# Attention heads of a two-layer block: a chunk's values and the emptying of their bank ahead of the slot's scores, in every engine's queue

## What is computed

```
def mla_attend(qn, qr, kn, kr, v):                       # 8 heads, kind "A"
    s = einsum('bqhd,bkhd->bhqk', qnb, kn) + einsum('bqhr,bkr->bhqk', qrb, kr)
    p = softmax(s * scale); return einsum('bhqk,bkhe->bqhe', p, v)
def diff_attend(q1, q2, k1, k2, v, lam):                 # 4 heads, kind "B"
    p = softmax(q1 k1^T * scale) - lam * softmax(q2 k2^T * scale)
    return einsum('bhqk,bkhe->bqhe', p, v)
for l in range(2):
    o_a = mla_attend(latent queries, context + latent keys)      # 768 keys
    o_b = diff_attend(latent queries, context + latent keys)
    if l == 0:  the same for the 256 context queries over 256 context keys
    o = branches, gates, w_out; then a convolutional feed-forward
```

## Time and profile before

| | |
|---|---|
| median of 3 runs | 3942.68 us (3940.96 to 3946.26) |
| the profiled execution | 3944.44 us, span of its instructions 3942.7 us |
| TensorE busy / VectorE / ScalarE | 89% / 48% / 37% of the span |
| mean granted TensorE clock | 0.938 of 2.4 GHz |
| heads of layer 0 | from about 150 to 636 us |
| heads of layer 1 | from about 1509 to 1967 us |

### The profile page before, as it was taken

How to read it: one execution, slowest core, us unless ns; L and a number is a source line. 1 busy time by engine, 2 the same in 40 slices (tenths; PEclk the granted TensorE clock), 3 DMA queues, 4 the chain that set the end, 5 groups by cost and what they waited for, 6 DMA issues and landing times.

```text
span 3942.7 us, 42589 instructions
## 1 busy us (share of the span) xinstructions
PE 3510.4 (89%) x17750; PEld 2934.2 (74%) x17750; DVE 1892.3 (48%) x2667; ACT 1443.6 (37%) x2201; POOL 312.0 (8%) x244
## 2 busy tenths in 40 slices
PE   7788998999999986788779999888999976979997
PEld 6667777888888875677667888766887765857886
DVE  5554555747635335445555645435333455334233
ACT  4443444233324243334423323434232344253222
POOL 0000000211001100000011101111001200230001
PEclk9999999999999998899899999999999867989999
DMA  5001014423321120011163332221222200212221
GB/s 194 33 19 57 32 54 156 157 96 123 109 79 65 59 73 32 5 57 45 64 219 128 124 109 90 92 78 67 98 100 91 77 1 11 79 51 86 101 91 65
DMA packets 74495, 321.96 MB, mean 82 GB/s; under 512 B 8896, under 2 KB 17856, under 8 KB 52288
## 3 DMA queue, kind: packets, MB, share of 16 engines
q1 hardware_dynamic: 74304, 319.25, 23.6%
HBM read 303.49 MB, written 15.73 MB: 81 GB/s over the span
## 4 chain that ended last, share of the span: by engine, by line
PE 68%; DVE 15%; ACT 9%; issue 3%; DMA 3%; POOL 2%; SPq 1%; POOLq 0%; ACTq 0%; DVEq 0%
PE psum L647 19%; PE psum L648 19%; PE psum L649 19%; DVE arena L1502 2%; DVE split_weights L618 2%; DMA arena<-w_ada_dram 2%; DVE arena L1434 2%; PE psum L1145 2%; ACT arena L1278 1%; POOL arena L1934 1%; ACT split_weights L607 1%; DVE split_high L1448 1%; PE psum L660 1%; PE psum L1171 1%; PE psum L661 1%
## 5 line engine op out<-in xcount | busy, mean ns | idle before, releaser
L647 PE MATMUL psum<-split_inputs,split_weights 128*128 128x512 f32 (+1 forms) x2936 | 1088.5, 371 | 18.8 <-DVE split_weights L618 14.4
L648 PE MATMUL psum<-split_inputs,split_weights 128*128 128x512 f32 (+1 forms) x2936 | 1076.8, 367 | 0.0
L649 PE MATMUL psum<-split_inputs,split_weights 128*128 128x512 f32 (+1 forms) x2936 | 1075.6, 366 | 0.0
L618 DVE TENSOR_TENSOR split_weights<-arena,split_weights 128x2048 fp32r<-128x2048 f32 (+3 forms) x246 | 508.1, 2067 | 405.7 <-ACT split_weights L607 405.4
L647 PEld LDWEIGHTS psum<-split_inputs,split_weights 128*128 128x128 f32 x2936 | 561.3, 191 | 115.3 <-DVE split_weights L618 16.3
L648 PEld LDWEIGHTS psum<-split_inputs,split_weights 128*128 128x128 f32 x2936 | 560.6, 191 | 90.9 <-issue 4.2
L649 PEld LDWEIGHTS psum<-split_inputs,split_weights 128*128 128x128 f32 x2936 | 559.5, 191 | 89.2
L607 ACT ACTIVATE split_weights<-arena 128x2048 fp32r<-128x2048 f32 (+3 forms) x246 | 413.6, 1682 | 176.4 <-PE psum L649 163.7
L647 PE MATMUL psum<-split_hidden,split_weights 128*128 128x512 f32 (+1 forms) x880 | 324.6, 369 | 0.6 <-DVE split_weights L618 0.5
L648 PE MATMUL psum<-split_hidden,split_weights 128*128 128x512 f32 (+1 forms) x880 | 324.3, 369 | 0.0
L649 PE MATMUL psum<-split_hidden,split_weights 128*128 128x512 f32 (+1 forms) x880 | 324.2, 368 | 0.0
(11 more groups left out here) (316 smaller groups left out, 5000.8 us busy)
## 6 DMA issues: line engine op xcount, KB each, us to landing
arena<-w_up_dram SPq DMA_DIRECT2D x44, 1024.0 KB, 4.8
arena<-ffn_up_dram SPq DMA_DIRECT2D x44, 1024.0 KB, 4.8
arena<-w_ada_dram SPq DMA_DIRECT2D x80, 512.0 KB, 3.8
arena<-w_in_dram SPq DMA_DIRECT2D x32, 1024.0 KB, 4.9
arena<-w_down_dram SPq DMA_DIRECT2D x32, 704.0 KB, 4.2
arena<-ffn_down_dram SPq DMA_DIRECT2D x32, 704.0 KB, 4.1
arena<-od_w_in_dram SPq DMA_DIRECT2D x13, 1024.0 KB, 4.9
arena<-w_ada_dram SPq DMA_DIRECT2D x8, 1024.0 KB, 12.7
```

What stands on the lines that cost most here:

```text
L618: dve.e.tensor_tensor(ws[:, i, 1, 0:nk * w], raw_view(key), ws[:, i, 0, 0:nk * w].bitcast(F32), ALU.subtract).then_inc(*w_lo(*key))
L647: pe.e.matmul(dst, a[0], b[0], start=i == 0, stop=False)
L648: pe.e.matmul(dst, a[0], b[1], start=False, stop=False)
L649: ins = pe.e.matmul(dst, a[1], b[0], start=False, stop=i == n - 1)
```

## The change

In the loop over slots, the two lines that emit a slot's first score and the weighing move from ahead of the values to behind them (and so behind `ob_sum`). Nothing is added or removed.

```diff
@@ head_items, for x, (i, c) in enumerate(slots) @@
         scores = plan[x]["scores"]
-        out += scores[0:1]
-        out += [("weigh", t) for t in weigh]
-        weigh = [t for _, t in scores if t in second]
         of_norm(x, "ob_sum")
         values.append((i, c))
         if len(values) > 2:
             of_values(x, *values.pop(0))
+        out += scores[0:1]
+        out += [("weigh", t) for t in weigh]
+        weigh = [t for _, t in scores if t in second]
         of_norm(x, "ob_root")
         out += gates[x]
```

## The result

The changed kernel takes **3876.98 us** (median of 4 runs, 3872.85 to 3878.43) against 3944.01 of the kernel before in the same comparison: ratio 0.9834, 95% interval 0.9821 to 0.9846, 67 us faster. The forecast was 3884 in a range of 3866 to 3914. The profiled execution took 3875.62 us, its span is 3873.9, 68.8 less than before, at a mean granted clock of 0.944.

The account below looks back on a forecast made before the run. With no engine full in layer 1's kind A heads, a loop through several engines, with TensorE waiting at L1171 for the bank, sets the pace; 31 + 5 + 10 + 13 = 59 us gained, forecast 3884 us, range 3866 to 3914.

Parts of the forecast that it names:

- the signs: Profile readings expected after the change, such as L1171's waits for L1460 falling from 77 to about 30 us.
- the three waits of 2.5: TensorE's three alike waits in layer 0's kind B, to be filled by L1171 and values: 6.6 us, each below 1.3.
- Kind A, layer 1: Heads of 27.1 us fall to 19.9 at full or 22.9 at half clock: 31 us gained (23 to 39).
- the emptying: ScalarE's bank copy and VectorE's two instructions after it, moved ahead of exponential and maximum: bank free 2.3 us earlier a pair.
- Kind A, layer 0: Heads of 24.0 us gain a net 0.8 each, ScalarE and VectorE handing to each other binding: 5 us (2 to 8).
- (a): ScalarE's and VectorE's part: bank freed ahead of exponential and maximum, 2.3 us earlier a pair, these two 0.86 us later.
- Kind B, layer 0: TensorE nearly full; values fill its waits, with some work behind them at full clock: 10 us gained (6 to 13).
- Kind B, layer 1: The 6.10 us wait shortens by 3.3, waits for L1465 go, values fill score waits: 13 us gained (8 to 17).
- Rival 1: In the heads, stretches behind shortened waits stay at half clock: 45 us gained, 3898 us; chance 0.23.
- Rival 2: The exponential becomes the bound everywhere, as in layer 0's kind A: 20 us gained, 3923 us; chance 0.14.
- Rival 3: Some 110 scores come late behind values and the emptying gains nothing: 15 us slower at most, 3958 us; chance 0.06.
- Rival 4: No change: the stage behind the heads takes their gain back, waiting for a DMA or a weight; chance 0.05.

Follow-up runs that it names:

- e2: Kernel before with only ScalarE's and VectorE's queues changed (bank emptied ahead of exponential and maximum), TensorE's order kept: 3905.78 us, ratio 0.9901.
- e4: Kernel before with all three queues changed, but only in layer 1's kind A slots: 3911.59 us, ratio 0.9912.
- e7: Changed kernel, but VectorE takes the maximum first as before and TensorE keeps the score ahead of values that begin a pair: 3904.88 us, ratio 0.9901.
- e5: Changed kernel, but on TensorE alone a slot's first score stays ahead of values that begin a pair: 3894.59 us, ratio 0.9872.
- e1: Kernel before with only TensorE's queue changed (values ahead of the score): 3961.62 us, ratio 1.0043.
- e6: Kernel before with only TensorE's queue changed, the score staying ahead of values that begin a pair: 3946.25 us, ratio 1.0011.
- e9: Changed kernel, but in layer 0's kind A VectorE takes the maximum first and TensorE keeps the score ahead of pair-beginning values: 3876.65 us, ratio 0.9830.
- e3: Changed kernel, but VectorE keeps its order of before, the maximum ahead of the two instructions that free the bank: 3908.77 us, ratio 0.9910.

## Why the prediction was right, and where not

- **The sum.** 59 us forecast, 67 measured, all four terms on the low side, none by more than 3.4. Most of the signs came: L1171's waits at 35.6 for about 30, layer 1's heads at 20.9 with a clock of 0.93, layer 0's at 23.1, the three waits of 2.5 at 1.3; VectorE's waits for scores, 25.4 in all, stayed below 30, and ScalarE waited at L1298 once, for 0.65 us.
- **Kind A, layer 1** (31 forecast, 33.2): right in kind and size. e2 shows that the emptying alone makes it, e4 that it is made within the stage. Heads take 20.9 us where 19.9 and 22.9 were reckoned at the full and the half clock. The clock rose to 0.93: 13.9 us of the 32.1 in that stretch.
- **Kind A, layer 0** (5, measured 6.4): the size right, the reason half right, and part of it luck. The net of 0.8 us a head does not follow from the numbers given with it: 1.05, less twice 0.86 with 0.4 given back, is 0.13. That an exponential later by the emptying costs time there is what e7 against e5 shows, 0.83 us each with the clock's part in it. But I took TensorE's order for harmless there; e1 and e6 show that alone it costs 20 us, since L1171 stands ahead of the score, and that (a) turns it into a gain (6.1, e5) once the wait is short.
- **Kind B, layer 0** (10, measured 13.4): the waits went as forecast (1.31, 1.35 and 1.35 left of the three of 2.50; the one of 7.2 became 7.99), idle time fell by 7.3 against some 9 reckoned. The mis-sized term is the clock behind the filled waits: 0.9 us forecast in all, 6.1 measured. e5 shows that it is the values in the waits that gain: without a pair's first values there, the stage has -4.2.
- **Kind B, layer 1** (13, measured 15.7): the wait of 6.10 became 2.70, 3.4 shorter against 3.3; those for L1465 outside the tail are gone. Idle time fell by 9.3 where about 12 was reckoned, and the clock again gave more, 6.4 against about 1.
- **Rival 1** (half clock) fell: it would have left kind A's stretch in layer 1 at 0.81. **Rival 2** (the exponential binds everywhere) fits kind A of layer 0 alone. **Rival 3** names a harm that is real in TensorE's order alone, of nearly that size, but by another way: e1 lies at 3962 where it said 3958, not by the length of the values ahead of 110 scores but by a waiting instruction ahead of two scores in a head. In the change its condition, an emptying that gains nothing, did not hold. It also took VectorE to wait for scores at about 9 places in layer 0; the kernel before has 6, with 12.2 us. **Rival 4** (no change) fell: the stretch between the layers moved by -0.4.
- **The change as two parts that add** was wrong. -18.9 and 43.3 do not make 68.3. The forecast did not use the sum of the two: it walked both parts together, stage by stage.

## What to carry to other kernels

When an item moves ahead of another in an in-order queue, ask what it waits for, not only how long it runs: the same swap was worth +6 or -20 us with the wait in front of it short or long. An edit to a shared list is several edits, one for each engine, and their gains need not add; try them apart before keeping or dropping the whole. And price a filled wait together with the clock behind it: here idle time and clock gave 44 and 24 us. A gain in one stage is safe only after the stage behind it has been read too: e9 won 6.8 us in one and lost 3.8 in the next.

## What the runs showed of the hardware

Shorter waits did not always keep the clock. In kind A of layer 0 the kernel before, with a wait of 2.78 us in every repeating head, had 0.99; the kernel after, with none longer than 1.9 in these heads, had 0.95, and e3 with waits up to 1.7 had 0.92 and 7.7 us more busy time for the same matmuls; e7, with waits up to 0.7, had 0.99. Nor does the idle time in all set it: it is 29.7, 20.8, 22.2 and 16.6 us in these four. In stretches of 3 us (length, busy time of TensorE, of its weight loads, of VectorE and of ScalarE, clock) the kernel before:

```profile
229.00:232.00 3.00, 0.84 (x6) 0.54 (x4) 1.54 (x3) 1.69 (x4) 0.00 (x0) 1.00 0.00 0
232.00:235.00 3.00, 2.39 (x14) 1.74 (x15) 1.99 (x4) 1.23 (x3) 0.00 (x0) 1.00 0.10 22
```

and the kernel after:

```profile
235.00:238.00 3.00, 1.53 (x13) 1.53 (x14) 1.62 (x5) 0.97 (x3) 0.00 (x0) 0.99 0.02 5
238.00:241.00 3.00, 3.00 (x14) 2.81 (x13) 1.88 (x5) 1.44 (x4) 0.00 (x0) 0.50 0.00 0
```

The first had more idle time and kept 2.4 GHz; the second fell to 1.2 GHz for the next 3 us. The Trainium skill (TensorE: Matmul & The Clock Gate, "HAM oscillation") has long waits as what starts a burst cold. Carried over to waits as short as these, which is my step and not the page's, it would make the kernel before the colder one. In layer 1 that direction agrees (0.81 to 0.93), in layer 0 the rows go the other way. What decides between the two patterns stays open: no run kept the waits and moved only their place.
